# Prompt attention of a hybrid decoder step: scores five jobs ahead, query tiles in sets of four, and a set's value products in one burst

## The reference

```python
def mla_scores(q_abs, q_rope, ckv, krope):
    s = (jnp.einsum('bqhr,bkr->bhqk', q_abs, ckv, preferred_element_type=jnp.float32)
         + jnp.einsum('bqhd,bkd->bhqk', q_rope, krope, preferred_element_type=jnp.float32))
    return s * ATT_SCALE

    def block(args):
        qa_b, qr_b, qp_b = args
        s = mla_scores(qa_b, qr_b, ckv, krope)
        s = jnp.where(pos[None, :] <= qp_b[:, None], s, -jnp.inf)
        p = jax.nn.softmax(s, axis=-1).astype(ckv.dtype)
        return jnp.einsum('bhqk,bkr->bqhr', p, ckv)
```

## Time and profile before

| | |
|---|---|
| median of 3 runs | 1772.34 us (1769.61 to 1776.97) |
| span of the profiled execution | 1763.0 us |
| PE busy | 1434.9 us (81%) |
| DVE busy | 931.7 us (53%) |
| ACT busy | 661.6 us (38%) |
| stage 2 | from about 508 to 1134 us of the span |

### The profile page before, as it was taken

How to read it: one execution, slowest core, us unless ns; L and a number is a source line. 1 busy time by engine, 2 the same in 40 slices (tenths; PEclk the granted TensorE clock), 3 DMA queues, 4 the chain that set the end, 5 groups by cost and what they waited for, 6 DMA issues and landing times. The chain is left out here.

```text
span 1763.0 us, 23574 instructions
## 1 busy us (share of the span) xinstructions
PE 1434.9 (81%) x7064; PEld 1114.7 (63%) x7064; DVE 931.7 (53%) x1531; ACT 661.6 (38%) x1517; POOL 531.0 (30%) x416
## 2 busy tenths in 40 slices
PE   5889798896637888887878788577677999999996
PEld 4667586763426666666666666445455788888884
DVE  3588787979536664665767566432222233333321
ACT  5242323332236664665667566400002222222210
POOL 4255273625104404042230404084001122222221
PEclk9999899997659998999999999878888999999998
DMA  7251423322162132121203212270504433332210
GB/s 239 76 189 33 165 68 130 102 84 87 38 118 64 27 84 60 35 61 33 74 16 81 61 35 63 50 192 25 120 0 149 127 95 95 95 95 81 80 45 29
DMA packets 153742, 145.55 MB, mean 83 GB/s; under 512 B 65557, under 2 KB 122486, under 8 KB 151926
## 3 DMA queue, kind: packets, MB, share of 16 engines
q1 hardware_dynamic: 146390, 119.50, 24.5%
q0 software_dynamic: 4384, 14.69, 2.6%
q10 hardware_dynamic: 2880, 10.49, 1.8%
HBM read 108.08 MB, written 47.04 MB: 88 GB/s over the span
## 5 line engine op out<-in xcount | busy, mean ns | idle before, releaser
L1077 PE MATMUL sc<-k,q 128*128 128x512 f32 (+2 forms) x960 | 273.3, 398 | 26.1 <-DVE k L1176 23.0
L1088 PE MATMUL tp<-ident,prob 128*128 128x128 f32 x1088 | 184.2, 287 | 103.3 <-ACT prob L1133 98.5
L1202 DVE TENSOR_TENSOR pT<-tp,pT 128x512 fp32r<-128x512 f32 (+2 forms) x320 | 194.6, 608 | 123.4 <-ACT pT L1143 122.8
L660 DVE SCALAR_TENSOR_TENSOR y<-aT,cols,y 128x512 f32<-128x512 f32 x240 | 240.2, 1001 | 18.1 <-DVE qst L735 6.6
L1143 ACT ACTIVATE pT<-tp 128x512 fp32r<-128x512 f32 (+2 forms) x320 | 170.7, 534 | 173.4 <-PE tp L1088 151.1
L1088 PEld LDWEIGHTS tp<-ident,prob 128*128 128x128 f32 x1088 | 128.3, 145 | 159.8 <-issue 86.0
L1133 ACT ACTIVATE prob<-sc,nm 128x512 f32<-128x512 f32 (+2 forms) x320 | 197.2, 621 | 28.7 <-DVE nm L1188 20.5
L1668 PE MATMUL m<-w_gate,hT 128*128 128x512 f32 x816 | 196.3, 399 | 10.5 <-POOL hT L1633 10.5
L1668 PE MATMUL m<-w_out,m 128*128 128x512 f32 (+1 forms) x816 | 196.7, 400 | 9.9 <-DVE m L1779 5.7
L1185 DVE TENSOR_REDUCE mx<-sc 128x1 f32<-128x512 f32 (+3 forms) x288 | 177.3, 616 | 45.1 <-PE sc L1077 29.9
L1077 PEld LDWEIGHTS sc<-k,q 128*128 128x128 f32 x960 | 160.7, 198 | 40.9 <-issue 27.1
(11 more groups left out here) (231 smaller groups left out, 1803.8 us busy)
## 6 DMA issues: line engine op xcount, KB each, us to landing
xtok<-in_x ACTq DMA_DIRECT2D x20, 512.0 KB, 4.3
qraw<-QT SPq DMA_DIRECT2D x9, 1024.0 KB, 5.4
xraw<-in_xT SPq DMA_DIRECT2D x17, 512.0 KB, 4.7
QT<-qst SPq DMA_DIRECT2D x32, 256.0 KB, 2.5
LAT<-in_cache_ckv SPq DMA_DIRECT2D x128, 64.0 KB, 2.2
lat<-LAT SPq DMA_DIRECT2D x16, 512.0 KB, 6.6
yt<-Y SPq DMA_DIRECT2D x16, 512.0 KB, 5.6
shared<-in_x SPq DMA_DIRECT2D x16, 512.0 KB, 4.1
```

Source lines behind the costliest of these rows:

```text
L660: dve.scalar_tensor_tensor(out, src, dw[:, c, k:k + 1], out, ALU.mult, ALU.add).then_inc(s["conv"], 1)
L1077: ins = pe.matmul(bank[:, 0:w], q2[:, hf, pw_, t * P:(t + 1) * P], k2[:, hf, px, c * GROUP:c * GROUP + w], start=(q == 0), stop=(q == 2 an ...
L1088: ins = pe.transpose(bank[:, k * P:(k + 1) * P], prob[:, t % 2, c * GROUP + k * P:c * GROUP + (k + 1) * P], ident[:, :])
L1202: dve.tensor_tensor(cut(1), bank[:, 0:w].rearrange("p (k q) -> p k q", q=P), f32(cut(0)), ALU.subtract)\
```

## The change

In the order of the diff:

- `LEAD` becomes 5: PE computes scores five jobs ahead, with the same five banks. A score product therefore waits for the exps of the job that is transposed in the same step.
- `EARLY` is 2: ACT computes exps two jobs ahead instead of one. `prob` becomes a ring of five chunks in place of two whole rows, and `mx` and `nm` get eight places instead of four.
- The values of a set are no longer cut into slices. All of them stand at PE's step `pair_end + 2`, two steps behind the transposes of the set's last job. hi of the next set's first job waits for the whole set (`pairs_done`).
- The second head of an iteration takes its sets in reversed order: four chunks first, one chunk last.
- SP and POOL count sets instead of groups; what they do in a set stays as it was.

The core of the diff:

```diff
-        LEAD = 4
+        LEAD, EARLY, RING, NM = 5, 2, 5, 8
-        prob = sb("prob", [P, 2, SEQ])
+        prob = sb("prob", [P, RING, GROUP])
+        pairs = [(0, p) for p in range(SETS)] + [(1, p) for p in reversed(range(SETS))]
...
+        items_at = {}
+        for q, (hf, p) in enumerate(pairs):
+            for k in range(4 * p + 4):
+                items_at.setdefault(min(pair_end[q] + 2, J), []).append((q, k))
...
-                    if t % 4 == 0:
-                        before = [e for e in ends if e < n]
-                        if before and c <= ends[before[-1]][1]:
-                            act.wait_ge(s["pv_done"], slices(i, before[-1], c))
+                    if t % 4 == 0 and c == 0:
+
+                        act.wait_ge(s["pv_done"], pairs_done(i, q - 1) if q else i * PT + 1)
...
-                    exps(i, 0)
+                    for n in range(EARLY):
+                        exps(i, n)
                     for n in range(J):
-                        new_tile = n + 1 < J and jobs[n + 1][2] == 0
-                        if n + 1 < J and not new_tile:
-                            exps(i, n + 1)
+                        ahead = n + EARLY
+                        begins = ahead < J and jobs[ahead][2] == 0
+                        if ahead < J and not begins:
+                            exps(i, ahead)
                         hi(i, n)
-                        if new_tile:
-                            exps(i, n + 1)
+                        if begins:
+                            exps(i, ahead)
```

More of the change, by code:

```diff
@@ L931, in stage2 @@
         zero = sb("zero2", [P, 1])
-        olo, ost = sb("olo", [VDIM, GROUP]), sb("ost", [VDIM, 2, GROUP])
+        olo, ost = sb("olo", [VDIM, SET]), sb("ost", [VDIM, 2, SET])
         ident_b, mask_b, mask_f = sb("ident_b", [P, P], BF16), sb("mask_b", [P, P], BF16), sb("mask_f", [P, P])
[L935 to L938, removed]
+        pairs = [(0, p) for p in range(SETS)] + [(1, p) for p in reversed(range(SETS))]
+        jobs, pair_of, pair_end = [], [], []
+        for q, (hf, p) in enumerate(pairs):
+            for t in range(4 * p, 4 * p + 4):
+                for c in range(t // 4 + 1):
+                    jobs.append((hf, t, c, min(GROUP, (t + 1) * P - c * GROUP), c == t // 4))
+                    pair_of.append(q)
+            pair_end.append(len(jobs) - 1)
+        J, JH = len(jobs), len(jobs) // 2
+        tile_no = [sum(last for *_, last in jobs[:n]) for n in range(J)]
+        items_at = {}
+        for q, (hf, p) in enumerate(pairs):
+            for k in range(4 * p + 4):
+                items_at.setdefault(min(pair_end[q] + 2, J), []).append((q, k))
         sc = Banks(sem, "sc", [ctx.enter_context(nc.psum_tensor(f"sc{i}", [P, GROUP], F32)) for i in range(5)], J)
         tr = Banks(sem, "tr", [ctx.enter_context(nc.psum_tensor(f"tp{i}", [P, GROUP], F32)) for i in range(2)], J)
-        pv = ctx.enter_context(nc.psum_tensor("pv", [P, GROUP], F32))
-        s = {n: sem(n) for n in ("const", "raw", "split", "head_done", "mx", "nm", "pT_hi", "pv_done", "pv_free", "olo", "ost",
-                                 "den", "init", "masks", "table", "gather", "first_hi", "first_lo", "turn", "krT_zero", "stage3")}
+        pv = ctx.enter_context(nc.psum_tensor("pv", [P, SET], F32))
+        s = {n: sem(n) for n in ("const", "raw", "split", "mx", "nm", "pT_hi", "pv_done", "pv_free", "olo", "ost",
+                                 "den", "init", "masks", "table", "gather", "first_hi", "first_lo", "turn", "krT_zero", "stage3", "o_begun")}
         landed = [sem(f"landed{i}") for i in range(5)]
@@ L949, in stage2, with pairs_done @@
         SP_N = 6
[L951 to L963, removed]
-        LEAD = 4
+        PT = len(pairs)
+        def pairs_done(i, q):
+            return i * PT + q + 2
         first = []
@@ L1007, in _ @@
                 with sp.Fori(0, HEADS // 2) as i:
[L1008 to L1016, removed]
+                    for q, (hf, p) in enumerate(pairs):
+                        if q % SETS == 0:
+                            sp.wait_ge(s["split"], i * 2 * SP_N + (2 + hf) * SP_N)
+                            load((i * 2 + 2 + hf) % HEADS)
+                        gather(i * 2 + hf, range(q % SETS * 4, q % SETS * 4 + 4))
+                        sp.wait_ge(s["ost"], i * PT + q + 1)
+                        sp.sem_inc(s["o_begun"], 1)
+                        sp.dma_start(a["Y"][bass.ds((i * 2 + hf) * VDIM, VDIM), p * SET:(p + 1) * SET],
+                                     ost[:, q % 2, :]).then_inc(o_out[q % 2], 16)
                 sp.wait_ge(s["krT_zero"], 1)
@@ L1029, in _ @@
                     pool.sem_inc(b, 16)
[L1030 removed]
+                pool.sem_inc(s["pv_done"], 1)
                 pool.sem_inc(s["pv_free"], 1)
@@ L1067, in scores @@
                     hf, t, c, w, last = jobs[n]
-                    if n % JH == 0 and hf:
+                    if n == JH:
                         pe.wait_ge(s["split"], i * 2 * SP_N + 2 * SP_N)
@@ L1087, in transposes, with values @@
                     for k in range(w // P):
-                        ins = pe.transpose(bank[:, k * P:(k + 1) * P], prob[:, t % 2, c * GROUP + k * P:c * GROUP + (k + 1) * P], ident[:, :])
+                        ins = pe.transpose(bank[:, k * P:(k + 1) * P], prob[:, n % RING, k * P:(k + 1) * P], ident[:, :])
                     ins.then_inc(tr.done[n % tr.n], 1)
[L1091 to L1109, removed]
+                def values(i, q, k):
+                    hf, p = pairs[q]
+                    if k == 0:
+                        if p == 0 and not hf:
+                            pe.wait_ge(s["first_lo"], 9)
+                        m = pair_end[q]
+                        pe.wait_ge(tr.free[m % tr.n], tr.count(i, m) + 1)
+                        pe.wait_ge(s["pv_free"], i * PT + q + 1)
+                    c0 = max(0, k - 4 * p) * P
+                    for part in range(2):
+                        ins = pe.matmul(pv[:, c0:], v2[:, hf, k, :], pT[:, part, k, c0:], start=(k == 0 and part == 0),
+                                        stop=(k == 4 * p + 3 and part == 1))
+                    if k == 4 * p + 3:
+                        ins.then_inc(s["pv_done"], 1)
                 with pe.Fori(0, HEADS // 2) as i:
@@ L1117, in _ @@
                         transposes(i, n)
[L1118 to L1121, removed]
+                        for q, k in items_at.get(n, ()):
+                            values(i, q, k)
+                    for q, k in items_at[J]:
+                        values(i, q, k)
             @block.scalar
@@ L1132, in exps @@
                     act.wait_ge(s["nm"], i * 2 * NT + tile_no[n] + 1)
-                    act.activation(prob[:, t % 2, c * GROUP:c * GROUP + w], bank[:, 0:w], ACT.Exp, bias=nm[:, t % 4:t % 4 + 1],
+                    act.activation(prob[:, n % RING, 0:w], bank[:, 0:w], ACT.Exp, bias=nm[:, tile_no[n] % NM:tile_no[n] % NM + 1],
                                    accum_out=dsum[:, hf, t, c:c + 1]).then_inc(sc.free[n % sc.n], 1)
@@ L1177, in _ @@
                 DN = 2 * 2
[L1179 to L1188, removed]
                 mxc, count = [], 0
@@ L1195, in _, with maxima @@
                 MXN = count
+                def maxima(i, n):
+                    hf, t, c, w, last = jobs[n]
+                    z = tile_no[n] % NM
+                    bank = sc.wait_done(dve, i, n)
+                    if last and c == 0:
+                        dve.reduce_max(nm[:, z:z + 1], bank[:, 0:w], AXX, negate=True).then_inc(s["nm"], 1)
+                        return
+                    dve.reduce_max(mx[:, z, c:c + 1], bank[:, 0:w], AXX).then_inc(s["mx"], 1)
+                    if last:
+                        dve.wait_ge(s["mx"], i * MXN + mxc[n])
+                        dve.reduce_max(nm[:, z:z + 1], mx[:, z, 0:c + 1], AXX, negate=True).then_inc(s["nm"], 1)
                 def lo(i, n):
                     hf, t, c, w, last = jobs[n]
+                    q = pair_of[n]
                     bank = tr.t[n % tr.n]
@@ L1203, in lo, with values @@
                        .then_inc(tr.free[n % tr.n], 1)
[L1205 to L1210, removed]
+                def values(i, q):
+                    hf, p = pairs[q]
+                    dve.wait_ge(s["olo"], i * PT + q + 1)
+                    dve.wait_ge(o_out[q % 2], i * (PT // 2 * 16) + (q // 2) * 16 + 16)
+                    dve.tensor_tensor(ost[:, q % 2, :], pv[0:VDIM, :], olo[:, :], ALU.add).then_inc(s["ost"], 1)
+                    dve.wait_ge(s["ost"], i * PT + q + 1)
                     dve.sem_inc(s["pv_free"], 1)
-                    if g == 3:
+                    if q % SETS == SETS - 1:
                         dve.reduce_sum(den[:, hf, :], dsum[:, hf, :, :], AXX).then_inc(s["den"], 1)
```

28 lines of the change are left out of this document (15 added, 13 removed).

## The result

The changed kernel takes 1791.04 us (median of 4 runs, 1788.96 to 1794.53) against 1770.97 us for the kernel before, measured beside it (median of 4, 1761.43 to 1776.97). The ratio is 1.0139, with a 95% interval of 1.0103 to 1.0175: it is slower, by 18 to 31 us. The two medians alone lie 20 us or 1.1% apart, inside this interval. The forecast was 1795 us, 1.3% slower.

The account below looks back on a forecast made before the run. Stage 2 was taken as bound by waits between PE, DVE and ACT, one loop through all three. Four iterations losing 4.8 us each plus 4.3 for SP make 23 on a 1763.0 span, 1786, plus 9.3 outside: 1795 us; range 1750 to 1820.

Parts of the forecast that it names:

- The seam: Between two sets in stage 2: ACT and DVE stand still for the whole burst, at 28 seams; a larger loss.
- Inside a set: Tiles within a set in stage 2: a small gain, some 0.4 us for a four-chunk tile.
- the clock: PE's granted rate in stage 2: no change taken, with 31 us open above and 17 us an iteration below.
- a sign of being right: Stage 2 profile: an iteration of 157 to 160 us, four-chunk first tiles 12 to 15 us, the others 5.3 to 5.9.
- the fourth rival: PE's clock goes down: a half-rate stretch at 16 or so larger seams, 2 us each, 1827 us; chance 0.06.
- The third rival: PE's clock comes back: products in one piece stay at 2.4 GHz, 1764 us; chance 0.18 together with no change.
- SP at the end: End of stage 2: SP, copying four pages first, issues the last write late, once in the program, 4.3 us.
- The iteration's start: First one-chunk set of an iteration in stage 2: set at 5.2 us.
- the one-chunk set and restart at its end: End of an iteration in stage 2: 13.6 us for the one-chunk set and 4.5 for the restart.
- time around the span: Outside the profiled span: the median stood 9.3 us above it, and the rest of the launch was put as unchanged.
- That the look-ahead frees DVE: Stage 2, first rival: DVE never waits for hi, four-chunk tiles take 5.1 us, 1747 us in all; chance 0.24.
- "No change": Second rival: seams cost 0.6 us less each, about 1778 us; chance 0.18 together with the third rival.

Follow-up runs that it names:

- e9: Changed kernel, but hi of the next set's first tile waits only for its own chunk's products; olo and ost not moved: ratio 0.9973 to the kernel before.
- e1: Changed kernel, burst kept, but hi waits only for its own chunk's products, and olo and ost come one step later: 1736 us, 0.9831 to the kernel before.
- e6: Kernel before, with slices and rising set order kept, but LEAD 5 and EARLY 2: ratio 0.9887 to the kernel before.
- e3: Changed kernel with LEAD 4 and EARLY 1 again and the burst one step behind the set's last job instead of two: ratio 1.0142 to the kernel before.
- e5: Changed kernel with scores of the third and fourth step behind each set's last job computed twice, keeping PE at work: ratio 1.0086 to the kernel before.
- e4: Changed kernel with the second head's sets in rising order again: ratio 1.0223 to the kernel before.

## Why the prediction was right

**The seam.** I had worked out 12.7 us for the first tile of a four-chunk set behind a burst of 24 products, and 14.7 behind one of 32; the profile has 12.4 and 14.5 to 14.6 in every iteration. For the three-chunk sets 8.3 and 12.2 were forecast and 8.2 and 11.9 measured, for the two-chunk ones 4.8 and 8.7 against 4.7 to 4.8 and 8.3. The wait of hi was to grow to some 150 us in 28 places, and is 152.7 in 28. That this wait is the cause, and not a companion, is shown by e9: only what hi waits for is changed, and the loss of 1.4% turns into a gain of 0.3%. With olo and ost moved too (e1) it is a gain of 1.7%.

**Inside a set.** Inner four-chunk tiles were forecast at 5.6 us and took 5.62 and 5.3 where the burst before them was far enough away; three-chunk tiles 4.0 to 4.1 against 4.06. Here e6 adds what I had left out: the look-ahead by itself gains 1.1%, or 5 us an iteration, of which the inner four-chunk tiles hold some 2. What it is worth with the burst is not shown, as e3 moves the burst along with it.

**The step that was mis-sized: the clock.** I took no change, as the same share of idling stays. It does not: behind the seams the idling gathers in PE's three gaps of 0.94 us, and the clock falls to half there. e5 gets 0.5% back, net of its own extra work, with stage 2 at 0.97 of full speed, which is above the 0.95 of before; what the fall from 0.95 to 0.94 cost by itself no run shows. Measured as in the prediction, over the last three iterations from olo to olo, the changed kernel takes (1159.95 - 678.85) / 3 = 160.4 us for an iteration and e5 157.5, against my 158.5:

```profile
678.85 0.60 ACT L1144 ACTIVATE olo<-pv 64x512 f32<-64x512 f32 x1 [3.50 <-PE pv L1102]
...
1159.95 0.59 ACT L1144 ACTIVATE olo<-pv 64x512 f32<-64x512 f32 x1 [3.50 <-PE pv L1102]
```

That is just above the 157 to 160 us that I had named as a sign of being right, and of the second tiles behind the seams of four-chunk sets, with 5.5 to 7.7 us, six in eight are above the 5.9 that I had named. So the fourth rival was part of the truth, at about a quarter of its price (9 of 32 us). The third rival, clock given back by bursts in one piece, fell: the stage is granted 0.94, not more than before. The Trainium skill ("TensorE: Matmul & The Clock Gate", on HAM oscillation) gives its advice for thin matmuls that would else wait for DMA. The trace agrees for the burst itself, whose 24 products took 4.94 us at a granted clock of 1.00; it differs on the whole: the waits here are for other engines, and the pause that a burst forces on them comes back as gaps on PE.

```profile
725.88:730.82 4.94, 4.94 (x27) 4.22 (x26) 0.07 (x1) 0.00 (x0) 0.00 (x0) 1.00 0.24 58
```

**SP at the end.** The last ost and the last write out stand here on the timeline:

```profile
1160.57 0.68 DVE L1207 TENSOR_TENSOR ost<-pv,olo 64x512 f32<-64x512 f32 x1 [3.40 <-ACT olo L1144]
...
1162.91 0.54 SPq L989 DMA_DIRECT2D LAT<-in_cache_ckv  x1
1163.71 0.52 SPq L991 DMA_DIRECT2D KR<-in_cache_krope  x1
1164.56 0.52 SPq L1017 DMA_DIRECT2D Y<-ost  x1
```

SP is still copying pages when ost is done, and issues the write 3.3 us behind it; 4.3 were forecast.

**Two smaller sizes.** The iteration's start was set at 5.2 us and takes 3.7 in all but the first; the one-chunk set and restart at its end were set at 18.1 and take 18.6 to 18.8. That the sum came out so near is luck in part: 1.5 us too much at the start of an iteration and 1 us too much for SP stand against what the clock took. And I read 9.3 us between the span of the profile and the median as time around the span. In the changed kernel the profiled run took 1792.24 us with a span of 1790.4, so that only 1.8 lie around it. If as much lies around the span of before, its profiled execution took some 1765 us, less than its median. It did no harm to the sum, which was one of differences.

**The other rivals.** That the look-ahead frees DVE fell for the changed kernel: lo's wait for hi grew from 122.8 us to 198.8. With slices it is half true: in e6 that wait is 94.0 us and the program gains, but the four-chunk tiles take 5.5 to 5.6 us, not the 5.1 of that rival. The rows are those of before and of e6:

```profile
DVE pT L1202 <- ACT pT L1143: 122.8, 134, 4.3
```

```profile
DVE pT L1204 <- ACT pT L1143: 94.0, 145, 4.1
```

"No change" fell with the interval.

## What to carry to other kernels

Before work is gathered into one burst, look at who waits for its end and what stands behind that waiter in its queue: here one wait on ACT stopped two engines for the whole burst, 28 times. A wait for the part that is needed, and moving the reader of the result one step back, made the program with the same burst 3.0% faster. Slices two steps behind, with that reader moved too, were 1.1% faster than slices right behind. Before a step is moved ahead, count which instruction frees the bank that it needs: here the fifth score bank was freed by the same exps as before, and PE's wait moved from the transposes to the scores.

## What the runs showed of the hardware

PE's clock followed gaps that the busy share of a stage hides. From 732.6 to 736.0 us PE worked 1.51 us, between three waits of 0.94, and the stretch up to 739.4 was granted 0.51, 1.2 GHz, in a stage that is 82% busy. With the scores done twice in two of these gaps (e5) the stretches at the same seam were granted 1.00, and the program was 0.5% faster, as far as the two intervals tell. And a stretch of transposes with gaps ahead of 32 products let the first 14 of these run at half the clock (e4).
